# Latent attention: the reciprocals of the softmax sums spread by fp32r products of ones with diagonal blocks

## The chip, the cores and the metric

The kernel is one launch on one core of a Trainium2 chip. What counts is the device time of that launch in microseconds (us). The engines are TensorE (PE in the profile, its weight loads PEld), VectorE (DVE), ScalarE (ACT), GpSimd (POOL) and SyncE (SP, which only starts transfers). Each runs its own list of instructions in order and waits for the others on semaphores.

## The reference

A two-layer backbone over 1024 latent and 256 context tokens of width 1024. Each layer has an input projection, three mixers side by side (a long convolution, a retention, latent attention), an output projection and an MLP. The change is in the attention. Per head (8 heads, keys of 96, values of 64) it computes

```python
s = jnp.einsum('bqhd,bkhd->bhqk', qi, k, preferred_element_type=jnp.float32)
p = jax.nn.softmax(s, axis=-1).astype(v.dtype)
return jnp.einsum('bhqk,bkhd->bqhd', p, v)
```

The latent queries see all 1280 keys. In the first layer alone the context queries are computed too, and they see the 256 context keys. Queries, keys and values of a head come from low-rank inputs by one more matrix product each (`w_uq`, `w_ukv`).

## The kernel before, in words

Every product in full precision is made of fp32r halves: a tensor is split into a high and a low part, and `three_pass` multiplies hi by hi, hi by lo and lo by hi (lines 152 to 154).

`phase_latent` does the attention of a layer. A **unit** is one tile of 128 queries of one head. The units run pair of heads by pair (p = 0 to 3), in it head by head (s = 0, 1), in it tile by tile: 10 tiles in the first layer (t = 8 and 9 are the context tiles, with two key tiles only), 8 in the second, so 80 and 64 units. Two neighbouring units are a **couple** (40 and 32 of them): they share one accumulation with the values. All engines walk over the same step number j, each a fixed distance behind:

- PE, step j: scores of unit j (`score`, lines 152 to 154 with kT and qT), transposes of the exponentials of units j-2 and j-1 (line 2031), and one half of `weigh` of the couple m: half 0 at j = 2m+4, half 1 at the odd step j = 2m+5 (line 2051, 10 products of 128x256 for latent tiles). At the end of half 1 it **spreads the reciprocals**: line 2059 multiplies the broadcast column of 1/sum with the identity, an fp32 product of 64x128 for each of the two units, so that every row of the output block has the reciprocals of its queries. Last it **makes** the next query, key or value chunk, if one stands in the table `made_in` (a deck of 12 makes for the pair to come in the first layer, `k k k q q q v v v q q q`, of 10 in the second). A make fills one of the four PSUM banks in a ring, and `bank_free` waits until what lay there has been read: for a make it is ACT's copy of the make before.
- DVE, step j: row maxima of unit j (line 1923, 1927), the low parts of the transposed probabilities (line 1943), and at odd j = 2m+3 `invert(m)`: the sums of couple m added and inverted (lines 1936 and 1937, names att_sums and att_rinv).
- ACT, step j: high parts of the transposed probabilities (line 1767), then `copy` of the make of step j-1 out of PSUM (line 1748, name make_raw, two buffers, so it waits until GpSimd is through with the make before the last), then at even j = 2m+6 `out(m)`: reciprocals and both value sums out of PSUM (lines 1775 to 1777), and `exp` of unit j (line 1757).
- POOL, step j: at even j = 2m+6 `norm(m)` (lines 1856, 1859), then `split` of the make of step j-1 into its high and low parts (lines 1823 to 1847), and at the third step of a pair `weights(p)`: the split of the raw weights of the next pair (lines 1806 to 1809).
- SP loads the raw weights of the pairs to come into one buffer, and stores the finished pair.

`out(m)` waits for `norm(m-1)`, `weigh` of the next couple waits for `out(m)`, and `score` of the next unit waits for `exp`.

Of the kernel before, what the change touches and what calls it, by code (L numbers as in the profile page):

```python
# [19 lines left out]
F32 = mybir.dt.float32  # L20
# [5 lines left out]
P = 128  # L26
# [1511 lines left out]
def latent_weights(kit, l, q, p):  # L1538
# [3 lines left out]
    uq_raw, ukv_raw = kit.at("uq_raw", [P, 2, LAT_QW], 187 if first else 130), kit.at("ukv_raw", [P, LAT_KVW], 191 if first else 132)  # L1542
# [14 lines left out]
def phase_latent(kit, l):  # L1557
# [15 lines left out]
    uq_raw = [kit.at("uq_raw", [P, 2, LAT_QW], kb) for kb in (187, 130)]  # L1573
    ukv_raw = [kit.at("ukv_raw", [P, LAT_KVW], kb) for kb in (191, 132)]
# [20 lines left out]
    mx = kit.at("att_max", [P, 2, 8], 202.5)  # L1595
    sums, rinv = kit.at("att_sums", [P, 2, SUM_RING], 202.75), kit.at("att_rinv", [P, SUM_RING], 203)
# [30 lines left out]
    for p in range(1, PAIRS):  # L1627
        deck = [("k", p, 0, c) for c in range(3)] + queries(p, 0) + [("v", p, 0, c) for c in range(3)] + queries(p, 1)
        made_in.update({(p - 1) * per_pair + 5 + i: m for i, m in enumerate(deck)})
# [46 lines left out]
    for s in (scored, exped):  # L1676
        s.plan(parts)
    p_turned, p_hi, p_lo = kit.sig("att_p_turned"), kit.sig("att_p_hi"), kit.sig("att_p_lo")
# [20 lines left out]
    with nc.Block() as block:  # L1699
        @block.sync  # L1700
        def _(sp):
            sp.dma_start(rot[MLA_NOPE:P, :], io["rope_rows"]).then_inc(rot_in.sem, 16)
            sp.wait_ge(kr_ready.sem, kr_ready["kr"])
            latent_weights(kit, l, sp, 1)
            n_tok = len(q_tiles) * P
            for p in range(PAIRS):
                if p + 2 < PAIRS:
                    sp.wait_ge(w_lo.sem, w_lo[p + 1])
# [83 lines left out]
        def _(pool):  # L1792
# [56 lines left out]

            def norm(m):  # L1850
# [11 lines left out]
            for j in range(n_units + 5):  # L1862
                if 0 <= j - 6 and j % 2 == 0:
                    norm((j - 6) // 2)
                    own(normed, normed[(j - 6) // 2])
                if j - 1 in made_in:
# [9 lines left out]
        def _(dve):  # L1876
            link = kit.dve_chain.link
            dve.wait_ge(w_hi.sem, w_hi["first"])
# [90 lines left out]
        def _(pe):  # L1969
# [65 lines left out]
            def weigh(m, half):  # L2035
# [17 lines left out]
                if half == 1:  # L2053

                    pe.wait_ge(inverted.sem, inverted[m])
                    r = s * MLA_V
                    for i in range(2):
                        at = (2 * m + i) % SUM_RING
                        last = pe.matmul(psf[r:r + MLA_V, O0 + (2 + i) * P:O0 + (3 + i) * P],
                                         rinv[:, at:at + 1].broadcast_to([P, MLA_V]), kit.ident[:], start=True, stop=True)  # L2060
# [1012 lines left out]
def build(nc, io, phases=None):  # L3073
    with ExitStack() as ctx:
# [6 lines left out]
        kit.ones = kit.small("ones", [P, P])  # L3081
# [6 lines left out]
        kit.ret_pos, kit.ret_lg = kit.small("ret_pos", [P, 4]), kit.small("ret_lg", [P, 8, DEPTH * 2 * RET_H])  # L3088
        kit.ret_dm_dram = nc.dram_tensor("ret_dm_scratch", (DEPTH, P, RET_H, P), F32).ap()
# [131 lines left out]
```

## Time and profile before

| | us |
|---|---|
| median of 3 runs | 3949.2 (3948.46 to 3953.78) |
| the profiled execution, own time | 3948.27 |
| its span in the profile | 3946.4 |
| PE busy (share of the span) | 3643.4 (92%) |
| DVE busy | 2129.9 (54%) |
| ACT busy | 1417.4 (36%) |
| POOL busy | 1366.5 (35%) |

PE is the busiest engine by far: read first where it waits and for whom. The profile is of one execution. Its own time is 1.9 us over its span and 0.9 us under the median. Attention takes about 655 to 1053 us in the first layer and 2626 to 2976 us in the second. A row of the trace gives a start, a duration, an engine, a line, and what is written and read; in square brackets stands how long the engine was idle before it and what ended that. PE's matmuls overlap: what one costs is the distance between two starts, not its duration.

### The profile page before, as it was taken

The page shows a single profiled execution, that of the slowest core. Times are in us where ns is not written, and L with a number is a line of the kernel's source. Part 1 is how long each engine was busy: PE and PEld are TensorE (multiplying, and loading weights), DVE is VectorE, ACT ScalarE, POOL GpSimd, SP SyncE. Part 2 cuts the span into 40 slices and gives each one's busy share as a digit, 9 for nine tenths or more (in the row PEclk, how much of TensorE's full clock was granted, in tenths as well). Part 3 has the DMA queues.
Part 4 walks back from the last instruction along what each step waited for, and adds up shares of the span by engine and source line. Part 5 has one row for each costly group of instructions (what it writes and reads, how often), then busy time and mean ns, then how long its engine had stood idle before and what let it go on. Part 6 is the DMA issues. An engine that isn't in the chain of part 4 may idle for free. (4 is left out here: it accounts for less than half of the span.)

```text
span 3946.4 us, 53247 instructions
## 1 busy us (share of the span) xinstructions
PE 3643.4 (92%) x19584; PEld 3058.6 (78%) x19584; DVE 2129.9 (54%) x3793; ACT 1417.4 (36%) x2845; POOL 1366.5 (35%) x1239
## 2 busy tenths in 40 slices
PE   7989997999779899999999899969996989999997
PEld 3668996777667688888888679958886768888886
DVE  5468435666676444444444583356676555544544
ACT  3341125666513522222222412246672252222222
POOL 1121122555100055454554421126630005544554
PEclk8989977999889999999999899879998999999999
DMA  5245201001324111111111162010014311111111
GB/s 206 104 168 186 82 4 41 12 8 40 122 78 163 43 43 32 32 43 43 43 32 32 69 202 79 4 39 10 6 39 165 150 43 50 52 48 43 53 52 49
DMA packets 153895, 266.96 MB, mean 68 GB/s; under 512 B 8968, under 2 KB 122777, under 8 KB 151290
## 3 DMA queue, kind: packets, MB, share of 16 engines
q1 hardware_dynamic: 143452, 212.38, 16.2%
q0 software_dynamic: 6352, 46.01, 3.0%
q10 hardware_dynamic: 3920, 6.29, 0.5%
q8 instruction: 107, 1.75, 0.2%
q14 instruction: 64, 0.52, 0.0%
HBM read 229.10 MB, written 33.59 MB: 67 GB/s over the span
## 5 line engine op out<-in xcount | busy, mean ns | idle before, releaser
L2990 POOL TENSOR_TENSOR x<-x,mlp_tmp 128x512 f32<-128x512 f32 x576 | 785.3, 1394 | 1323.7 <-DVE mlp_tmp L2971 1318.5
L2971 DVE TENSOR_TENSOR mlp_tmp<-psum,gate 128x512 f32<-128x512 f32 x576 | 391.7, 689 | 273.1 <-POOL x L2990 194.5
L152 PE MATMUL psum<-act_hi,w_hi 128*128 128x512 f32 (+1 forms) x1280 | 472.6, 369 | 14.4 <-DVE w_lo L2949 14.4
L153 PE MATMUL psum<-act_lo,w_hi 128*128 128x512 f32 (+1 forms) x1280 | 472.3, 369 | 0.0
L154 PE MATMUL psum<-act_hi,w_lo 128*128 128x512 f32 (+1 forms) x1280 | 472.1, 369 | 0.0
L152 PE MATMUL psum<-w_hi,hidden_hi 128*128 128x512 f32 x1152 | 449.9, 391 | 0.0
L153 PE MATMUL psum<-w_lo,hidden_hi 128*128 128x512 f32 x1152 | 448.5, 389 | 0.0
L154 PE MATMUL psum<-w_hi,hidden_lo 128*128 128x512 f32 x1152 | 448.3, 389 | 0.0
L2963 DVE TENSOR_TENSOR hidden_lo<-square,hidden_hi 128x512 fp32r<-128x512 f32 x160 | 102.3, 639 | 591.9 <-ACT hidden_hi L2935 591.9
L1923 DVE TENSOR_REDUCE att_max<-psum 128x1 f32<-128x512 f32 (+2 forms) x272 | 217.4, 799 | 259.7 <-PE psum L154 259.5
L2927 ACT ACTIVATE relu<-psum 128x512 f32<-128x512 f32 x160 | 88.8, 555 | 666.0 <-PE psum L154 666.0
L152 PEld LDWEIGHTS psum<-act_hi,w_hi 128*128 128x128 f32 x1280 | 242.2, 189 | 56.0 <-DVE w_lo L2949 15.2
L1757 ACT ACTIVATE probs<-psum,att_max 128x512 f32<-128x512 f32 (+2 forms) x272 | 208.5, 771 | 190.5 <-DVE att_max L1927 189.8
L153 PEld LDWEIGHTS psum<-act_lo,w_hi 128*128 128x128 f32 x1280 | 242.2, 189 | 40.6
L154 PEld LDWEIGHTS psum<-act_hi,w_lo 128*128 128x128 f32 x1280 | 242.2, 189 | 40.3
L152 PE MATMUL psum<-w_in_hi,act_hi 128*128 128x256 f32 (+1 forms) x912 | 259.2, 284 | 0.0
L154 PE MATMUL psum<-w_in_hi,act_lo 128*128 128x256 f32 (+1 forms) x912 | 256.8, 282 | 0.0
L153 PE MATMUL psum<-w_in_lo,act_hi 128*128 128x256 f32 (+1 forms) x912 | 256.8, 282 | 0.0
L152 PEld LDWEIGHTS psum<-w_hi,hidden_hi 128*128 128x128 f32 x1152 | 216.3, 188 | 47.6 <-DVE mlp_tmp L2971 3.6
L154 PEld LDWEIGHTS psum<-w_hi,hidden_lo 128*128 128x128 f32 x1152 | 216.3, 188 | 45.2
L153 PEld LDWEIGHTS psum<-w_lo,hidden_hi 128*128 128x128 f32 x1152 | 216.4, 188 | 43.7
L2923 ACT ACTIVATE w_hi<-w_raw 128x1024 fp32r<-128x1024 f32 x64 | 64.2, 1051 | 467.5 <-PE psum L154 467.5
(386 smaller groups left out, 8238.6 us busy)
## 6 DMA issues: line engine op xcount, KB each, us to landing
w_raw<-in_mlp_w SPq DMA_DIRECT2D x128, 512.0 KB, 3.8
side_w<-in_w_ada SPq DMA_DIRECT2D x40, 1024.0 KB, 6.5
w_raw<-in_w_in SPq DMA_DIRECT2D x32, 512.0 KB, 4.8
hy_ahead<-in_hy_ahead POOLq DMA_DIRECT2D x8, 2048.0 KB, 12.6
open_tab<-in_hy_ahead POOLq DMA_DIRECT2D x8, 1024.0 KB, 13.0
spec_scratch<-open_staged SPq DMA_DIRECT2D x16, 512.0 KB, 2.7
hy_spec<-spec_scratch SPq DMA_DIRECT2D x16, 512.0 KB, 3.5
hy_back<-in_hy_back POOLq DMA_DIRECT2D x2, 4096.0 KB, 29.9
```

Of the source, the lines that this page charges most:

```text
L152: pe.matmul(out, lhs[0], rhs[0], start=start, stop=False)
L153: pe.matmul(out, lhs[0], rhs[1], start=False, stop=False)
L154: return pe.matmul(out, lhs[1], rhs[0], start=False, stop=stop)
L1757: act.activation(pe_[:, n % 2, at:end], psf[:, at:end], ACT.Exp, scale=SCALE, bias=mx[:, n % 2, 1:2], accum_out=sums[:, k, n % SUM_RING:n ...
L1923: dve_last = dve.tensor_reduce(mx[:, n % 2, 6 + k:7 + k], psf[:, at:at + len(part) * P], AX.X, ALU.max)
L2923: act.activation(w2h[:, f], raw2[:, f], ACT.Copy).then_inc(w2_hi.sem, 1)
L2927: act.activation(relu[:, i % 2, 0:n], ps[:, i % 4, 0:n], ACT.Relu).then_inc(relued.sem, 1)
L2963: dve.tensor_tensor(hlo[:, g % 2, f, 0:n], square[:, i % 2, 0:n], hh[:, g % 2, f, 0:n].bitcast(F32), ALU.subtract).then_inc(h_lo.sem, 1)
L2971: dve.tensor_tensor(tmp[:, j % 2, :], ps[:, 4 + j % 4, :], gate[:, int(t >= LAT_TILES), 512 * h:512 * h + 512], ALU.mult).then_inc(gated.s ...
L2990: pool.tensor_tensor(a, a, tmp[:, j % 2, :], ALU.add).then_inc(added.sem, 1)
```

## The change

The two fp32 products of the reciprocals become two fp32r products over both units at once. GpSimd prepares them: `spread(m)` multiplies the identity with each of the two columns of reciprocals (two blocks of 128x128 in one new buffer, `att_diag_full`), copies the 128x256 result into an fp32r high part and subtracts for the low part. PE multiplies a constant matrix of ones with the high and then with the low part. It now waits for `spread(m)` rather than for `invert(m)`. `spread(m)` stands at POOL's odd step j = 2m+3, ahead of the split of that step, and waits for `invert(m)` and for the end of `weigh(m-1)`, since there is one pair of diagonal buffers.

The decks of makes start one step later (6 + i rather than 5 + i). Buffers are moved: the raw weights lie on the bytes that `split` uses for its temporaries, so SP now loads a pair's raw weights only when the last query of the pair before it is split. Maxima, sums, reciprocals and the ones move to the small area, and DVE writes the ones at the start of the phase.

```diff
-    uq_raw = [kit.at("uq_raw", [P, 2, LAT_QW], kb) for kb in (187, 130)]
-    ukv_raw = [kit.at("ukv_raw", [P, LAT_KVW], kb) for kb in (191, 132)]
+    uq_raw = [kit.at("uq_raw", [P, 2, LAT_QW], kb) for kb in (187, 133)]
+    ukv_raw = [kit.at("ukv_raw", [P, LAT_KVW], kb) for kb in (191, 130)]
...
-    mx = kit.at("att_max", [P, 2, 8], 202.5)
-    sums, rinv = kit.at("att_sums", [P, 2, SUM_RING], 202.75), kit.at("att_rinv", [P, SUM_RING], 203)
+    mx, sums, rinv = kit.att_max, kit.att_sums, kit.att_rinv
+    diag = [kit.at(f"att_diag{a}", [P, 2, P], 202 + a, F32R) for a in range(2)]
+    diag_full = kit.at("att_diag_full", [P, 2, P], 131)
...
-        made_in.update({(p - 1) * per_pair + 5 + i: m for i, m in enumerate(deck)})
+        made_in.update({(p - 1) * per_pair + 6 + i: m for i, m in enumerate(deck)})
...
-            sp.wait_ge(kr_ready.sem, kr_ready["kr"])
+            sp.wait_ge(lo_p.sem, lo_p[weights_free(1)])
             latent_weights(kit, l, sp, 1)
...
                 if p + 2 < PAIRS:
-                    sp.wait_ge(w_lo.sem, w_lo[p + 1])
+                    sp.wait_ge(lo_p.sem, lo_p[weights_free(p + 2)])
                     latent_weights(kit, l, sp, p + 2)
...
+            def spread(m):
+                hi, lo = diag
+                at = 2 * m % SUM_RING
+                pool.wait_ge(inverted.sem, inverted[m])
+                if m:
+                    pool.wait_ge(weighed.sem, weighed[m - 1])
+                for i in range(2):
+                    link(pool, pool.tensor_scalar(diag_full[:, i, :], kit.ident[:], rinv[:, at + i:at + i + 1], None, ALU.mult))
+                link(pool, pool.tensor_copy(hi[:], diag_full[:]))
+                pool.tensor_tensor(lo[:], diag_full[:], hi[:].bitcast(F32), ALU.subtract).then_inc(spread_out.sem, 1)
...
+                if 0 <= j - 3 and j % 2 == 1 and j - 2 < n_units:
+                    spread((j - 3) // 2)
+                    own(spread_out, spread_out[(j - 3) // 2])
...
+            link(dve, dve.memset(kit.ones_r[:].bitcast(F32), 1.0))
...
-                    pe.wait_ge(inverted.sem, inverted[m])
-                    r = s * MLA_V
-                    for i in range(2):
-                        at = (2 * m + i) % SUM_RING
-                        last = pe.matmul(psf[r:r + MLA_V, O0 + (2 + i) * P:O0 + (3 + i) * P],
-                                         rinv[:, at:at + 1].broadcast_to([P, MLA_V]), kit.ident[:], start=True, stop=True)
+                    pe.wait_ge(spread_out.sem, spread_out[m])
+                    for a in range(2):
+                        last = pe.matmul(psf[:, O0 + 2 * P:O0 + 4 * P], kit.ones_r[:],
+                                         diag[a][:].rearrange("p i n -> p (i n)"), start=a == 0, stop=a == 1)
                     last.then_inc(weighed.sem, 1)
```

What this moves on PE is seen at the end of step j = 7 of the first layer, where the second half of `weigh(1)` ends. The kernel before:

```order
L2051 MATMUL psum<-probsT_hi_6435,v_parts_6427 128x256
L2051 MATMUL psum<-probsT_lo_6437,v_parts_6427 128x256
L2059 MATMUL psum<-ident,att_rinv_6445 64x128 x2
L152 MATMUL psum<-lat_hi_6143,w_ukv_hi_6420 128x256
L153 MATMUL psum<-lat_lo_6144,w_ukv_hi_6420 128x256
L154 MATMUL psum<-lat_hi_6143,w_ukv_lo_6421 128x256
```

The same place in the changed kernel:

```order
L2070 MATMUL psum<-probsT_hi_6439,v_parts_6431 128x256
L2070 MATMUL psum<-probsT_lo_6441,v_parts_6431 128x256
L2076 MATMUL psum<-att_diag_95_6447,ones_r 128x256
L2076 MATMUL psum<-att_diag_96_6448,ones_r 128x256
L152 MATMUL psum<-lat_hi_6147,w_ukv_hi_6424 128x512
L153 MATMUL psum<-lat_lo_6148,w_ukv_hi_6424 128x512
L154 MATMUL psum<-lat_hi_6147,w_ukv_lo_6425 128x512
```

The two products per couple stay two, of another kind. The make behind them is the second key chunk (512 wide) where it was the third (256 wide): the deck stands one step later.

On POOL the first deck of the first layer begins after `norm(0)` (L1856, L1859). The kernel before, from there to the second norm:

```order
L1856 TENSOR_TENSOR att_o_hi_6440<-att_o_hi_6440,att_o_lo_6441 64x256
L1859 TENSOR_TENSOR att_6426<-att_o_hi_6440,att_rec_6442 64x256
L1830 CAST kT_hi_6424<-make_raw_6431 64x512
L1831 TENSOR_TENSOR kT_lo_6425<-make_raw_6431,kT_hi_6424 64x512
L1832 CAST make_hi_6433<-make_raw_6431 64x512
L1833 CAST kT_hi_6424<-make_hi_6433 64x512
L1834 TENSOR_TENSOR kT_lo_6425<-make_raw_6431,make_hi_6433 64x512
L1830 CAST kT_hi_6424<-make_raw_6430 64x512
```

The same place in the changed kernel:

```order
L1871 TENSOR_TENSOR att_o_hi_6444<-att_o_hi_6444,att_o_lo_6445 64x256
L1874 TENSOR_TENSOR att_6430<-att_o_hi_6444,att_rec_6446 64x256
L1861 TENSOR_SCALAR att_diag_full_6449<-ident,att_rinv 128x128 x2
L1862 CAST att_diag_95_6447<-att_diag_full_6449 128x256
L1863 TENSOR_TENSOR att_diag_96_6448<-att_diag_full_6449,att_diag_95_6447 128x256
L1833 CAST kT_hi_6428<-make_raw_6435 64x512
L1834 TENSOR_TENSOR kT_lo_6429<-make_raw_6435,kT_hi_6428 64x512
L1835 CAST make_hi_6437<-make_raw_6435 64x512
L1836 CAST kT_hi_6428<-make_hi_6437 64x512
L1837 TENSOR_TENSOR kT_lo_6429<-make_raw_6435,make_hi_6437 64x512
L1871 TENSOR_TENSOR att_o_hi_6444<-att_o_hi_6444,att_o_lo_6445 64x256
```

The first spread of the program has one more row ahead of it. Two steps before the place above, in the split of the first pair's queries, the changed kernel's POOL has:

```order
L1850 TENSOR_TENSOR qT_lo_6427<-make_raw_6435,qT_hi_6426 96x512
L1861 ISA
L1861 TENSOR_SCALAR att_diag_full_6449<-ident,att_rinv 128x128 x2
L1862 CAST att_diag_95_6447<-att_diag_full_6449 128x256
L1863 TENSOR_TENSOR att_diag_96_6448<-att_diag_full_6449,att_diag_95_6447 128x256
L1849 CAST qT_hi_6426<-make_raw_6434 96x256
```

The spread stands ahead of the first key split, and one stands ahead of every second split of a deck. The row `ISA` occurs once at line 1861; the kernel before has one of the same kind at line 564, and the profile calls it MODIFY_POOL_CONFIG.

## Rows read from the trace of the kernel before

**Rows 1.** Windows view, 100 us of attention: span, PE, PEld, DVE, ACT, POOL.

```profile
700.00:800.00 100.00, 92.69 (x607) 78.30 (x607) 61.02 (x126) 65.96 (x166) 58.83 (x70) 1.00 0.04 12
```

**Rows 2.** PE's timeline, second layer: end of an odd unit without a make.

```profile
2906.39 0.28 PE L2051 MATMUL psum<-probsT_lo,v_parts 128*128 128x256 f32 x1
2906.60 0.65 PE L2059 MATMUL psum<-ident,att_rinv 128*64 128x128 f32 x4
2907.18 0.50 PE L152 MATMUL psum<-kT_hi,qT_hi 96*128 96x512 f32 x1
```

**Rows 3.** PE's timeline, second layer: starts of the two units before.

```profile
2898.01 0.50 PE L152 MATMUL psum<-kT_hi,qT_hi 96*128 96x512 f32 x1
...
2902.36 0.50 PE L152 MATMUL psum<-kT_hi,qT_hi 96*128 96x512 f32 x1
```

**Rows 4.** ACT's timeline, second layer: start of an `out`, head s = 1.

```profile
2908.82 0.38 ACT L1775 ACTIVATE att_rec<-psum 64x256 f32<-64x256 f32 x1
```

**Rows 5.** POOL by form: one-input and two-input operations; the last column is idle before.

```profile
L1806 POOL CAST w_ukv_hi<-ukv_raw 128x256 fp32r<-128x256 f32 x6 | 2.4, 396 | 0.4
L1807 POOL CAST w_uq_hi<-uq_raw 128x512 fp32r<-128x512 f32 x6 | 3.7, 614 | 0.4
L1808 POOL TENSOR_TENSOR w_ukv_lo<-ukv_raw,w_ukv_hi 128x256 fp32r<-128x256 f32 x6 | 4.4, 736 | 0.5
L1042 POOL CAST lat_hi<-lat_tmp 128x256 fp32r<-128x256 f32 x2 | 1.6, 805 | 2.2 <-ACT lat_tmp L976 2.1
```

**Rows 6.** POOL's timeline, first layer: starts of splits and norms, steps 6 to 16.

```profile
689.01 0.60 POOL L1830 CAST kT_hi<-make_raw 64x512 fp32r<-64x512 f32 x1
...
693.75 0.65 POOL L1830 CAST kT_hi<-make_raw 64x512 fp32r<-64x512 f32 x1
...
700.12 0.39 POOL L1830 CAST kT_hi<-make_raw 64x256 fp32r<-64x256 f32 x1
...
703.12 1.28 POOL L1841 TENSOR_TENSOR make_turned<-make_raw,rope_rows 32x512 f32<-32x512 f32 x1
...
709.23 0.73 POOL L1856 TENSOR_TENSOR att_o_hi<-att_o_hi,att_o_lo 64x256 f32<-64x256 f32 x1
...
710.85 1.26 POOL L1841 TENSOR_TENSOR make_turned<-make_raw,rope_rows 32x512 f32<-32x512 f32 x1
...
742.86 0.73 POOL L1856 TENSOR_TENSOR att_o_hi<-att_o_hi,att_o_lo 64x256 f32<-64x256 f32 x1 [1.91 <-ACT att_o_lo L1777]
```

**Rows 7.** PE's timeline: make of j=6, make of j=7, score(14).

```profile
688.94 0.40 PE L152 MATMUL psum<-lat_hi,w_ukv_hi 128*128 128x512 f32 x1
...
694.88 0.39 PE L152 MATMUL psum<-lat_hi,w_ukv_hi 128*128 128x256 f32 x1
...
726.77 0.44 PE L152 MATMUL psum<-kT_hi,qT_hi 96*128 96x512 f32 x1
```

**Rows 8.** ACT's timeline: copy, exp (j=13), out, exp (j=20).

```profile
723.47 0.62 ACT L1748 ACTIVATE make_raw<-psum 128x512 f32<-128x512 f32 x1
...
725.67 0.69 ACT L1757 ACTIVATE probs<-psum,att_max 128x512 f32<-128x512 f32 x1 [1.57 <-DVE att_max L1927]
...
757.40 0.38 ACT L1775 ACTIVATE att_rec<-psum 64x256 f32<-64x256 f32 x1
...
760.17 0.69 ACT L1757 ACTIVATE probs<-psum,att_max 128x512 f32<-128x512 f32 x1 [1.62 <-DVE att_max L1927]
```

**Rows 9.** ACT's timeline, second layer: exp (j=13), idle time before.

```profile
2698.88 0.69 ACT L1757 ACTIVATE probs<-psum,att_max 128x512 f32<-128x512 f32 x1 [2.08 <-DVE att_max L1927]
```

**Rows 10.** Line 564's pool configuration, and POOL's timeline around its first.

```profile
L564 POOLq MODIFY_POOL_CONFIG  x2: 7/7/7, 59.6 to 59.6; - x2
...
64.43 1.26 POOL L564 TENSOR_TENSOR open_ksum<-open_ksum,open_size 128x512 f32<-128x512 f32 x1 [4.79 <-DVE open_size L658]
```

**Rows 11.** Raw weights' DMA (last number: us to landing); POOL's last query split.

```profile
ukv_raw<-in_mla_w_ukv SPq DMA_DIRECT2D x3, 128.0 KB, 3.6
...
672.23 0.39 POOL L1846 CAST qT_hi<-make_raw 96x256 fp32r<-96x256 f32 x1
```

More of the change, by code:

```diff
@@ L1541, in latent_weights @@
     first = p == 0
-    uq_raw, ukv_raw = kit.at("uq_raw", [P, 2, LAT_QW], 187 if first else 130), kit.at("ukv_raw", [P, LAT_KVW], 191 if first else 132)
+    uq_raw, ukv_raw = kit.at("uq_raw", [P, 2, LAT_QW], 187 if first else 133), kit.at("ukv_raw", [P, LAT_KVW], 191 if first else 130)
     w_raw = kit.sig("lat_w_raw", 16)
@@ L1677, in phase_latent @@
         s.plan(parts)
+    spread_out = kit.sig("att_spread")
+    spread_out.plan(range(n_couples))
     p_turned, p_hi, p_lo = kit.sig("att_p_turned"), kit.sig("att_p_hi"), kit.sig("att_p_lo")
@@ L3080, in build @@
         kit.stat = kit.small("stat", [P, 4, 20])
-        kit.ones = kit.small("ones", [P, P])
+        kit.ones = kit.small("ones", [P, 8])
         kit.mla_gain = kit.small("mla_gain", [P, 3])
@@ L3088, in build @@
         kit.ret_pos, kit.ret_lg = kit.small("ret_pos", [P, 4]), kit.small("ret_lg", [P, 8, DEPTH * 2 * RET_H])
+        kit.att_max, kit.att_sums, kit.att_rinv = (kit.small(n, s) for n, s in (
+            ("att_max", [P, 2, 8]), ("att_sums", [P, 2, 8]), ("att_rinv", [P, 8])))
+        kit.ones_r = kit.small("ones_r", [P, P], F32R)
         kit.ret_dm_dram = nc.dram_tensor("ret_dm_scratch", (DEPTH, P, RET_H, P), F32).ap()
```

## The prediction

> **What bounds the kernel now.** I read the windows of the attention first: in 100 us of the first layer PE is busy 92.7 us, ACT 66, DVE 61, POOL 59 [rows 1]. PE bounds, but with gaps, so I read its timeline unit by unit, and then the engines that end its gaps. Two sorts of units without a make show. The odd unit from 2902.36 to 2907.18 takes 4.82 us, the even one before it 4.35 [rows 2, 3]. In the odd one PE works through and ends with line 2059. In the even one it waits near the end for ACT's exponentials: its length is the loop of score, maximum, exp and the next score, and PE's work is not its limit. So work taken off PE counts only in odd units. In units with a make (a deck is 12 of 20 units in the first layer, 10 of 16 in the second) PE takes up the slack, and ACT still idles 1.6 to 2.1 us ahead of its exp, waiting for the maximum [rows 8, 9]. Between those moments stands POOL: in the first deck it goes from split to split without a gap (689.01, 693.75, 700.12 after a norm, 703.12 [rows 6]), and a split begun late would hold ACT's copies. That is where the change has to be weighed.
>
> **PE, the products.** From the last product of line 2051 to the next score are 0.79 us [rows 2]. Neighbouring 128x256 products in that accumulation start 0.12 apart, so line 2059 costs 0.67 per couple. The new pair is two fp32r products with 256 columns, of the form of its neighbours: 0.24. That is 0.43 less per couple, 72 couples, at most 31.0 us. Three couples of the first layer and one more at its end stand behind context units, where the odd unit is already down to 4.34: nothing to win (-1.7). In the heads with s = 1, ACT's move of the output stands just before the exp of the even unit (2908.82 [rows 4]); with an odd unit that is shorter, ACT comes to that exp later in the unit, and part is given back. I estimate 0.12 per couple of s = 1, which makes 4.2 over 35 of them. Left are **-25.1 us**: 14.1 in the first layer, 11.0 in the second. That is the price if nothing else is late.
>
> **POOL, the spread.** No spread is in the trace. One-input operations took 0.396 us for 128x256 and 0.614 for 128x512, so 0.85 ns per element of a row; 128x128 would be 0.29 [rows 5]. Two of them 0.58, the copy 0.40, the subtraction 0.74, four gaps of 0.08: **2.1 us per couple**. From below: at half the 128x256 row each, 1.9. From above: tensor_scalar reads a scalar per partition, which no row shows; at half the two-input row it is 0.37 each, which gives 2.2. The dearest row of a 128x256 copy is 0.805 [rows 5]; with the first three operations at that height (two at 0.4 and one at 0.8, the blocks scaled) and the subtraction at 1.2 it comes to 3.1. I take 2.1, since most rows of POOL in this phase stand at the low price. POOL has 41 us free in 100 and gets about 20 us more work. The mean is not the question; the decks are.
>
> **The first layer's decks.** Anchor: the end of `weigh(1)` at j = 7, the make behind it starts at 694.88 [rows 7]. `spread(2)` of j = 7 must wait for just this (one pair of diagonal buffers), and behind it in POOL's order stands the split of K chunk 0, now made at j = 6. From the rows 6: K 512 wide 4.74, K 256 wide 3.0, a query split 6.1, a norm 1.6. POOL from the anchor: 0.3 until it starts, spread 2.1, K0 4.74, norm 1.6, K1 4.74, spread 2.1, K2 3.0, norm 1.6, Q0 6.1, spread 2.1, Q1 6.1: 34.5 us, with no gap to catch up in. ACT's copy of V0, at j = 13, has two raw buffers and must wait for the split of Q1. It takes 0.6, and exp(13) stands behind it. score(14) follows exp(13) by 1.1 (725.67 to 726.77 [rows 7, 8]). So score(14) stands at anchor + 36.3. Before it was 726.77 - 694.88 = 31.9, and PE alone would make it 30.4 (three couples less 0.43, and 0.2 from the key chunks' other places). The loss against PE alone is **5.9 us a deck**. In the kernel before, that copy began at 723.47, ahead of exp by 2.2, and waited for nobody.
>
> A second place is j = 20. `out(7)` waits for `norm(6)`, which stands in POOL's order at j = 18, behind Q0 and Q1 of the other head with a spread between them. From the norm at 742.86 [rows 6]: 1.6, 6.1, 2.1, 6.1, 1.6 = 17.5, so 760.4 where `out` began at 757.40 [rows 8]: 3.0 late. From its end to exp(20) were 1.6 free (758.6 to 760.17), so 1.4 reach score(21), and the two gains of the couples in between, 0.8, are lost too: 2.2. Together 8.1 per deck, 24.3 in three decks. First layer: 24.3 - 14.1 = **+10.2**.
>
> **The second layer's decks.** The same chain of 34.5 applies, but there are no short context units at j = 8 and 9, so ACT's slots lie later, and 2.1 us of slack stood ahead of the exp at j = 13 [rows 9]. I find the copies at most 2.3 late, of which about 0.75 passes through: 2.3 in three decks. Second layer: 2.3 - 11.0 = **-8.7**.
>
> **The rest.** A norm or a spread that comes later is not waited for elsewhere: `weigh` needs its spread two units after the maximum, 3 us of slack or more in the first layer, 0.8 in the second. In the first steps the spread of j = 3 goes ahead of the last query split (672.23 [rows 11]), and SP loads the next raw weights only after this split: 672.2 + 2.1 + 1.2 = 675.5, landing 3.6 [rows 11] and issue 0.9, 3.2 for POOL's weight splits: 683.2, while PE's K0 make is due at about 688.5 [rows 7]. The pool configuration at line 1861 is new. Line 564 has one: set at 59.6, and POOL's next operation at 64.43, just after DVE's [rows 10]. So it costs between 0 and 4.8; with 4.8 the weights are ready at 688.0, still in time. I put 0.5 for this and for DVE's write of the ones, between 0 and 3. In the later pairs the raw weights come 10 steps ahead of their use.
>
> The Trainium skill, "GPSIMD Engine Reference", § 2.1 Instruction dispatch, says that the first call into a freshly loaded library pays some 6 us for its code. The trace bounds it to 4.8 here. By the page the weights would be 1.2 later than by my upper bound, about 0.7 us of stall once; nothing of the sum changes its sign by it.
>
> **Sum.** +10.2 - 8.7 + 0.5 = +2.0 against the profiled execution's 3948.3: 3950.3. The median of the runs stands 0.9 above that execution: **3951.2 us**. It is a small difference of two large terms. The chain on POOL may be off by 1 us per deck, the gain on PE by 0.08 per couple, 6 us each: own range 3942 to 3961.
>
> **Rivals.**
> (1) POOL hides the spread. The decks' delays are taken up by ACT's and DVE's idle time, because copies and `out` can slip inside a unit. For it: POOL is free 41% of the time, and ACT idles 1.6 ahead of exp(13). Against it: that idle time is a third of the delay, and POOL has no gap in the deck. Time: 3948.3 - 25.1 + 0.5 + 0.9 = 3924.6; halfway, 3938.
> (2) The spread is dearer, and this ends slower. POOL's chain carries three spreads in a deck of the first layer and about 2.5 in one of the second, where the slack is then used up: 16.5 us of time for each us of price. From 2.5 us per spread the kernel is slower by more than the bound. At the upper end of 3.1 the time is 3951.2 + 16.5 = 3968. For it: the copy of 0.805 [rows 5], and POOL's operations would be beside more DVE work. Against it: the splits' copies in attention stand at 0.60 for 512 columns [rows 6].
> (3) The fp32r pair costs what line 2059 costs, as it waits for its weights or for the spread. Then the gain goes and the decks stay: about 3975. The neighbours of the same form at 0.12 speak against it.
>
> **How the numbers follow.** No change is within 0.2%, 7.9 us: 3941.3 to 3957.1. The forecast has 0.56 (0.02 of it faster, 0.42 the same, 0.12 slower). Rival 1 has 0.22, 0.20 of it faster and 0.02 the same. Rival 2 has 0.18: 0.16 slower, 0.02 the same. Rival 3 has 0.04, slower. Sum: faster 0.22, same 0.46, slower 0.32. The range takes in the halfway case of rival 1 and rival 2 up to 3.0: 3936 to 3967.
>
> **What the profile will show.** The new products start 0.12 apart, 144 of them, and the odd unit without a make falls from 4.82 to 4.39. The spread's four operations take 2.1 us from start to end. POOL's busy time in 100 us of the first layer goes from 59 to about 80. ACT's copies (none waited for POOL before) wait for it at j = 10, 12 and 13 of the first layer's decks, and `out` at j = 20. A period of the first layer (20 units) becomes longer by about 3.4 us where it has a deck, one of the second (16 units) shorter by about 2. I am wrong if copies at j = 13 do not wait, if the spread takes over 2.5 us, or if the odd unit does not fall.

## The result, and the profile after

| | before | changed |
|---|---|---|
| median of 6 runs, us | 3950.6 (3948.5 to 3953.8) | 3973.8 (3965.5 to 3980.5) |
| ratio, 95% interval | | 1.0057 (1.0041 to 1.0073) |
| span of the profiled execution | 3946.4 | 3976.1 |
| first layer, score(0) to score(79) | 387.0 | 414.5 |
| second layer, score(0) to score(63) | 333.2 | 334.2 |

The kernel became slower by 23 us, 0.6%. The profiled execution shows 29.7 us more, and all but 1.1 of it lies in the two attention stretches: 27.6 in the first layer, 1.0 in the second. They are measured on PE's timeline, from the start of the first score of the first unit to that of the last. The six times of the changed kernel lie in two groups, 3965.5 to 3969.7 us and 3977.9 to 3980.5 us, the first at a slightly higher mean clock (0.942 to 0.945 against 0.939), and the profiled execution is of the second, 4 us above the median.

The windows of 100 us, in the columns of [rows 1] (the number behind POOL's is the granted clock, 1.00 for 2.4 GHz), for the changed kernel; the last is a stretch of 6 us behind a stall:

```profile
700.00:800.00 100.00, 86.64 (x529) 75.80 (x530) 54.28 (x112) 59.73 (x149) 76.32 (x101) 0.91 0.03 11
819.00:825.00 6.00, 5.82 (x19) 5.05 (x20) 0.00 (x0) 2.66 (x7) 5.33 (x10) 0.50 0.00 0
```

POOL went from 59 to 76 of 100 us and PE from 93 to 87. The granted clock, 1.00 before, is 0.91 in the mean, and in the six microseconds behind a wait it is 0.50, which is 1.2 GHz. Over the whole first stretch TensorE ran at 1.2 GHz for 64 us in this execution (mean granted clock 0.92), against 10 us in the kernel before (0.99).

POOL's instructions by form, the spread's three lines:

```profile
L1861 POOL TENSOR_SCALAR att_diag_full<-ident,att_rinv 128x128 f32<-128x128 f32 x144 | 87.1, 605 | 153.2 <-DVE att_rinv L1956 80.5 <-PE psum L2076 63.4
L1863 POOL TENSOR_TENSOR att_diag<-att_diag_full,att_diag 128x256 fp32r<-128x256 f32 x72 | 52.7, 733 | 6.2
L1862 POOL CAST att_diag<-att_diag_full 128x256 fp32r<-128x256 f32 x72 | 28.6, 397 | 4.9
```

A tensor_scalar of 128x128 took 0.605 us. I had 0.29 from the copies [rows 5] and 0.37 as the upper estimate from two-input rows. The other two are as forecast. A spread is 2.6 us, not 2.1.

The second deck of the first layer on POOL's timeline. Only the row that begins each piece stands here (spread, key split, norm, key split, spread, short key split, norm, query split, spread, query split, norm):

```profile
803.88 1.30 POOL L1861 TENSOR_SCALAR att_diag_full<-ident,att_rinv 128x128 f32<-128x128 f32 x2 [5.49 <-PE psum L2076]
...
806.52 0.61 POOL L1833 CAST kT_hi<-make_raw 64x512 fp32r<-64x512 f32 x1
...
811.26 0.73 POOL L1871 TENSOR_TENSOR att_o_hi<-att_o_hi,att_o_lo 64x256 f32<-64x256 f32 x1
...
812.87 0.60 POOL L1833 CAST kT_hi<-make_raw 64x512 fp32r<-64x512 f32 x1
...
817.61 1.30 POOL L1861 TENSOR_SCALAR att_diag_full<-ident,att_rinv 128x128 f32<-128x128 f32 x2
...
820.25 0.39 POOL L1833 CAST kT_hi<-make_raw 64x256 fp32r<-64x256 f32 x1
...
823.25 0.72 POOL L1871 TENSOR_TENSOR att_o_hi<-att_o_hi,att_o_lo 64x256 f32<-64x256 f32 x1
...
824.86 1.26 POOL L1844 TENSOR_TENSOR make_turned<-make_raw,rope_rows 32x512 f32<-32x512 f32 x1
...
830.97 1.30 POOL L1861 TENSOR_SCALAR att_diag_full<-ident,att_rinv 128x128 f32<-128x128 f32 x2
...
833.63 1.27 POOL L1844 TENSOR_TENSOR make_turned<-make_raw,rope_rows 32x512 f32<-32x512 f32 x1
...
839.70 0.71 POOL L1871 TENSOR_TENSOR att_o_hi<-att_o_hi,att_o_lo 64x256 f32<-64x256 f32 x1
```

The first spread waits 5.49 us for the products of `weigh` before it, and behind it POOL goes for 36 us without a gap: the chain of the prediction, piece by piece. ACT's timeline where it waits for this chain (the copies of Q0 at j = 10 and V0 at j = 13, `out` at j = 20, in the second period):

```profile
817.60 0.60 ACT L1751 ACTIVATE make_raw<-psum 128x512 f32<-128x512 f32 x1 [4.56 <-POOL kT_lo L1837]
...
839.71 0.60 ACT L1751 ACTIVATE make_raw<-psum 128x512 f32<-128x512 f32 x1 [3.49 <-POOL qT_lo L1850]
...
876.04 0.38 ACT L1778 ACTIVATE att_rec<-psum 64x256 f32<-64x256 f32 x1 [3.19 <-POOL att L1874]
```

They answer to [rows 8], where none waits for POOL. And PE's timeline behind the first of them, from the stall to where the clock is back:

```profile
819.18 0.58 PE L2070 MATMUL psum<-probsT_hi,v_parts 128*128 128x256 f32 x1 [3.21 <-ACT att_o_lo L1780]
...
823.61 0.63 PE L154 MATMUL psum<-lat_hi,w_uq_lo 128*128 128x512 f32 x1
824.04 0.63 PE L152 MATMUL psum<-kT_hi,qT_hi 96*128 96x512 f32 x1
...
825.53 0.40 PE L153 MATMUL psum<-kT_lo,qT_hi 96*128 96x512 f32 x1
825.76 0.39 PE L154 MATMUL psum<-kT_hi,qT_lo 96*128 96x512 f32 x1
```

PE waits 3.21 us, and its products of 512 columns then follow each other at 0.43 us (823.61 to 824.04), against 0.23 once the clock is back (825.53 to 825.76). That costs time which the wait itself does not show.

What the change was to bring is there as well. PE's timeline at the end of an odd unit of the second layer, the place of [rows 2]:

```profile
2982.79 0.28 PE L2070 MATMUL psum<-probsT_lo,v_parts 128*128 128x256 f32 x1
2982.91 0.40 PE L2076 MATMUL psum<-att_diag,ones_r 128*128 128x256 f32 x2
2983.14 0.48 PE L152 MATMUL psum<-kT_hi,qT_hi 96*128 96x512 f32 x1
```

From the last product of `weigh` to the next score are 0.35 us where there were 0.79.

### The profile page after: what moved, and what is told of

Its sections match the earlier page's. It is cut to its first block and busy times, and to the rows that moved or that the text cites. A ratio compares the mean times of both kernels' runs of the same rounds, so it can differ in the third digit from the quotient of the medians.

```text
span 3976.1 us, 53327 instructions
## 1 busy us (share of the span) xinstructions
PE 3633.5 (91%) x19440; PEld 3063.9 (77%) x19440; DVE 2124.9 (53%) x3795; ACT 1422.2 (36%) x2845; POOL 1540.3 (39%) x1527
## 5 line engine op out<-in xcount | busy, mean ns | idle before, releaser
L154 PEld LDWEIGHTS psum<-w_hi,hidden_lo 128*128 128x128 f32 x1152 | 216.3, 188 | 45.1
```

The lines of the kernel that those rows point to most:

```text
L154: return pe.matmul(out, lhs[1], rhs[0], start=False, stop=stop)
```

## The experiments

Theory A was that POOL's spread makes the splits of the decks late, and that the clock adds to each stall. The rivals: B, the later decks and the moved loads are what costs; C, the new products save nothing; E, it is the amount of POOL's work and not its place; D, DVE's work lengthens the loop of score, maximum and exp. All intervals below are of the ratio to the kernel before, from runs on the same chip; the rows come from several chips, on which the kernel before had 3949.5 to 3951.3 us. The two stretches are of one profiled execution each. "First" and "second" are the two attention stretches, as in the table above.

| kernel | median us | ratio, 95% interval | first | second |
|---|---|---|---|---|
| changed | 3973.8 | 1.0041 to 1.0073 | 414.5 | 334.2 |
| decks later only | 3951.0 | 0.9993 to 1.0012 | 385.3 | 333.3 |
| no spread | 3919.4 | 0.9900 to 0.9933 | 369.4 | 321.6 |
| one product on POOL | 3947.0 | 0.9986 to 1.0005 | 394.6 | 324.0 |
| spread behind the split | 3949.5 | 0.9988 to 1.0007 | 397.6 | 320.3 |
| both of these | 3932.4 | 0.9935 to 0.9964 | 382.3 | 320.0 |
| PE's waits filled | 3965.3 | 1.0029 to 1.0063 | 401.4 | 332.7 |
| POOL's spread, old products | 3981.4 | 1.0062 to 1.0091 | 410.7 | 337.3 |
| spread on DVE | 3992.0 | 1.0096 to 1.0139 | 414.8 | 346.6 |
| two wide fp32r products | 3964.6 | 1.0019 to 1.0047 | 398.3 | 335.6 |
| one wide fp32 product | 3921.1 | 0.9917 to 0.9950 | 373.9 | 322.8 |
| the same, with a copy | 3919.8 | 0.9912 to 0.9939 | 372.7 | 322.8 |

**Decks later only.** In the kernel before:

```diff
-        made_in.update({(p - 1) * per_pair + 5 + i: m for i, m in enumerate(deck)})
+        made_in.update({(p - 1) * per_pair + 6 + i: m for i, m in enumerate(deck)})
```

> The kernel before with its decks one step later (6 + i for 5 + i) and nothing else. Theory A (the spread on POOL makes the splits late, and TensorE runs at half clock behind the stalls): no difference, 3946 to 3955 us. Theory B (the later deck is what costs, the spread only comes with it): 3960 to 3975 us, with ACT's copies at j = 13 waiting for POOL here too.

3951.0 us, no difference. B has lost its first half: the step by which the decks are later costs nothing by itself.

**No spread.** The changed kernel, with POOL's call of `spread` gone and

```diff
+            for a in range(2):
+                link(dve, dve.memset(diag[a][:].bitcast(F32), 1.0))
...
-                    pe.wait_ge(spread_out.sem, spread_out[m])
+                    pe.wait_ge(inverted.sem, inverted[m])
```

> The changed kernel with its later decks, moved buffers and fp32r products, but POOL writes no diagonal: DVE sets both buffers to 1.0 once, so the reciprocals are left out of the output, and the products wait for invert. Theory A: the gain on PE alone; couples without a make 8.6 us for 9.15 before, no copy waits for POOL, granted clock 1.00 in the decks, 3915 to 3928 us. Theory B (later decks, later weight loads): the stalls stay, 3955 to 3975 us. Theory C (the new products themselves cost as much as the old): 3945 to 3955 us.

3919.4 us, with the reciprocals left out of the output. B and C are both out: with later decks, later weight loads and the new products, the kernel is 30 us faster than before. The two stretches are 29.2 us shorter (17.6 and 11.6). So what the products give is 29 us, and what the spread on POOL takes is 45.1 + 12.6 = 58 us.

**One product on POOL.**

```diff
-                for i in range(2):
-                    link(pool, pool.tensor_scalar(diag_full[:, i, :], kit.ident[:], rinv[:, at + i:at + i + 1], None, ALU.mult))
+                link(pool, pool.tensor_tensor(diag_full[:], bcast(kit.ident[:], 1, 2), bcast(rinv[:, at:at + 2], 2, P), ALU.mult))
```

> The changed kernel with one POOL tensor_tensor of 128x256 (identity and reciprocals both repeated by stride 0) where two tensor_scalar of 128x128 stood: two operations of 0.605 and a gap become one of about 0.73, so a spread takes 2.1 us for 2.65. Theory A: 0.55 us less per spread in POOL's chain is 1.6 per deck of the first layer and its stalls (3.2, 2.0, 2.9 us) each get shorter by about as much: 3953 to 3966 us. Theory B: no change against the changed kernel, 3968 to 3980 us.

3947.0 us: better than expected by 6 us or more, and level with the kernel before. The product is cheaper than I expected. POOL's timeline of this kernel, one spread and what follows:

```profile
704.09 0.61 POOL L1860 TENSOR_TENSOR att_diag_full<-ident,att_rinv 128x256 f32<-128x256 f32 x1
704.77 0.40 POOL L1861 CAST att_diag<-att_diag_full 128x256 fp32r<-128x256 f32 x1
705.24 0.72 POOL L1862 TENSOR_TENSOR att_diag<-att_diag_full,att_diag 128x256 fp32r<-128x256 f32 x1
706.03 0.40 POOL L1833 CAST kT_hi<-make_raw 64x256 fp32r<-64x256 f32 x1
```

The one product of 128x256 took 0.61 us, as long as each tensor_scalar of half its size, so this spread is 1.94 us (704.09 to 706.03), 0.70 under the changed kernel's 2.64 and 0.16 under what I had predicted for the change. The loss against no spread falls from 45.1 to 25.2 in the first layer and from 12.6 to 2.4 in the second, 30 us in the two profiled executions and 24 us by the ratios of all runs, for 0.70 us of a spread. Theory A holds, but I had the slope too small.

**Spread behind the split.** The two calls in POOL's step change places:

```diff
-                if 0 <= j - 3 and j % 2 == 1 and j - 2 < n_units:
-                    spread((j - 3) // 2)
-                    own(spread_out, spread_out[(j - 3) // 2])
                 if j - 1 in made_in:
                     split(made_in[j - 1])
                     own(lo_p, lo_p[made_in[j - 1]])
+                if 0 <= j - 3 and j % 2 == 1 and j - 2 < n_units:
+                    spread((j - 3) // 2)
+                    own(spread_out, spread_out[(j - 3) // 2])
```

> The changed kernel with POOL's spread behind the split of its odd step, not ahead of it. POOL's chain loses one of three spreads ahead of V0's copy and starts 3 us earlier, since the split of K0 no longer waits for the end of weigh(1). Theory A: the waits of the first layer's decks shrink by 3 to 5 us each, 3940 to 3962 us. Rival E (what hurts is the amount of POOL work, not where it stands): 3968 to 3980 us. A third outcome: TensorE's products wait for the diagonals in the decks, since a split of 6 us now stands ahead of them.

3949.5 us, inside what theory A gave, and against E: the same instructions in another order take 24 us less. The second layer's loss is gone (320.3 against 321.6 without a spread). In the first layer units 12 and 13 still take 8.8 and 7.6 us.

**Both together.** The one product and the changed places, 3932.4 us:

> Both repairs of POOL's part together: the spread of three operations (one product of 128x256, 2.1 us) and behind the split of its step. Each alone took 24 to 27 us off the changed kernel and left waits in the first layer alone (394.6 and 397.6 us there against 369.4 without a spread). Theory A: POOL's chain in a deck is 0.56 shorter three times and starts earlier, most waits are gone: 3922 to 3940 us. If the wait of units 12 and 13 (8.8 and 7.6 us with the spread behind the split) is for the diagonals behind Q's split, it stays: 3942 us or more.

It is faster than the kernel before by 0.5%. PE's timeline in the second deck shows what is left: `out` is late at 815.62, and at 822.26 the products wait for the diagonals themselves.

```profile
815.62 0.39 PE L2069 MATMUL psum<-probsT_hi,v_parts 128*128 128x256 f32 x1 [1.28 <-ACT att_o_lo L1780]
...
822.26 0.51 PE L2075 MATMUL psum<-att_diag,ones_r 128*128 128x256 f32 x2 [1.16 <-POOL att_diag L1862]
```

**PE's waits filled.** In the first layer, ahead of the wait for `out` at j = 10 of each deck (24 products) and at j = 20 and 40 (22):

```diff
+            def fill(j, count):
+                item = ring[ring_at[(j - 1, min(1, len(turned_parts(j - 1)) - 1))] + 1]
+                bank_free(item)
+                for _ in range(count):
+                    pe.matmul(bank_of(item)[:, 0:256], kit.ones_r[:], ch[:, 2, 0:256], start=True, stop=True)
```

> The changed kernel, and TensorE has 24 (steps 10 of each deck) or 22 (steps 20 and 40) products of 128x256 into the next free bank of the ring to do where it stood idle for 3 us waiting for ACT's out, in the first layer only; nothing reads them. They are work of 2.9 and 2.6 us that only replaces idle time. Theory A with the clock (the stalls cost more than their length, since the granted clock is 1.2 GHz for 5 to 6 us behind each): the clock stays at 2.4 GHz behind them, units 20 and 21 get 2 to 3 us shorter per place, of the deck's part some is hidden by POOL: 3956 to 3968 us. Without it (the low clock costs nothing, all is POOL's chain): 3973 us or more.

3965.3 us, inside what the theory with the clock gave. That number alone shows no gain: the interval of its ratio, 1.0029 to 1.0063, overlaps the changed kernel's, 1.0041 to 1.0073. What the filling does is read from the places themselves. PE does 116 more products there. Windows of this kernel and then of the changed one, the 10 us that hold the wait at j = 20:

```profile
760.00:770.00 10.00, 9.66 (x72) 9.03 (x71) 4.85 (x12) 4.15 (x12) 7.93 (x12) 1.00 0.13 39
```

```profile
760.00:770.00 10.00, 7.09 (x49) 6.60 (x48) 4.68 (x11) 5.35 (x16) 9.14 (x12) 0.86 0.06 11
```

The clock stays at 1.00 where it fell to 0.86. Units 20 and 21 take 10.4 us for 13.0, and so do units 40 and 41, the same place one pair later; without a spread they take 8.3. So of 4.7 us lost at each such place 2.6 are the clock's, and 2.1 are POOL's chain. At j = 10 the filling only moves the wait to unit 12 (8.4 to 8.8 us for 4.9 to 5.9): from the make of j = 7 to score(14) the later decks take 38.4 us with it and 38.2 without. What is gained there is 0.9 us a deck, unit 14 back at full clock (5.3 us for 6.3), and 2.4 us in the first deck, where the clock had also been low in unit 13.

The first stretch is 13 us shorter in all, but the five filled places account for only 9 of it. Another 3.0 us is unit 4, ahead of all of them (4.35 us for 7.30). Both kernels do the same there, and PE waits 1.2 us for the exponentials in both, but the clock fell in one execution only:

```profile
671.60 0.77 PE L152 MATMUL psum<-kT_hi,qT_hi 96*128 96x512 f32 x1 [1.20 <-ACT probs L1760]
```

```profile
673.01 0.50 PE L152 MATMUL psum<-kT_hi,qT_hi 96*128 96x512 f32 x1 [1.21 <-ACT probs L1760]
```

The first row is of the changed kernel, the second of the one with filled waits. The waits at j = 13 and at j = 60 were not filled.

**POOL's spread, old products.**

```diff
-                    pe.wait_ge(spread_out.sem, spread_out[m])
+                    pe.wait_ge(inverted.sem, inverted[m])
```

and the two fp32 products of line 2059 below it.

> The changed kernel's POOL spread, decks and buffers, with TensorE's two fp32 products of before, which wait only for invert: nobody reads the diagonals. Loss without gain. Theory A: the couples outside the decks go back to 9.15 us for 8.62, and in the decks POOL is the bound and PE's work counts little: 3980 to 4000 us. If gain and loss only add: 3974 + 29 = 4003 us.

3981.4 us, only 7.6 over the changed kernel, with intervals that overlap (1.0062 to 1.0091 against 1.0041 to 1.0073): the difference may be anything from nothing to 16 us. It is not the 29 us of the sum, so gain and loss do not add. The products give 29 us without the spread, and at most about half of that beside it. The stretches are of no help here: the profiled execution of this kernel was its shortest (span 3970.9), that of the changed kernel one of its longer ones.

**The price of tensor_scalar.** One run, which leaves the reciprocals of the even units out of the output:

```diff
-                for i in range(2):
-                    link(pool, pool.tensor_scalar(diag_full[:, i, :], kit.ident[:], rinv[:, at + i:at + i + 1], None, ALU.mult))
+                link(pool, pool.tensor_scalar(diag_full[:, 0, :], kit.ident[:], 0.001, None, ALU.mult))
+                link(pool, pool.tensor_scalar(diag_full[:, 1, :], kit.ident[:], rinv[:, at + 1:at + 2], None, ALU.mult))
```

> Of the changed kernel's two POOL tensor_scalar of 128x128 the first takes a constant as its scalar (so the reciprocals of even units are left out of the output), the second a column, as before. If the column costs, the first takes 0.3 us, as copies of POOL do per element, and the second 0.605; if the operation itself is dearer than a copy, both take 0.6. The time is of no matter: near the changed kernel's, or 10 to 20 us less if the first is cheap.

It took 3969.2 us, inside the range of the changed kernel's times. Its POOL instructions by form:

```profile
L1861 POOL TENSOR_SCALAR att_diag_full<-ident,att_rinv 128x128 f32<-128x128 f32 x72 | 43.3, 602 | 6.8
L1860 POOL TENSOR_SCALAR att_diag_full<-ident 128x128 f32<-128x128 f32 x72 | 38.1, 530 | 139.4 <-DVE att_rinv L1957 78.8 <-PE psum L2077 58.1
```

The larger part of the price is the operation's and not the column's: 0.530 with a constant, 0.602 with a column of SBUF. Per element of a row this is 4.7 ns, against 2.9 for a product of two tiles (0.733 for 256) and 1.5 for a copy (0.397 for 256).

This kernel is the changed one but for 0.08 us per spread, and its profiled execution had 37 us at 1.2 GHz in the first stretch where the changed kernel's had 64. That stretch took 405.1 us against 414.5. At 34 us per us of spread, the slope found below, 0.08 makes about 3 us (an estimate), so some of the 414.5 belongs to that one execution and not to the kernel.

**Spread on DVE.** POOL's spread goes, DVE does after its reciprocal:

```diff
+                for i in range(2):
+                    link(dve, dve.tensor_scalar(hi[:, i, :], kit.ident[:], rinv[:, at + i:at + i + 1], None, ALU.mult))
+                for i in range(2):
+                    last = dve.scalar_tensor_tensor(out=lo[:, i, :], in0=kit.ident[:], scalar=rinv[:, at + i:at + i + 1],
+                                                    in1=hi[:, i, :].bitcast(F32), op0=ALU.mult, op1=ALU.subtract)
```

> The changed kernel with the spread on DVE behind its reciprocal: two tensor_scalar of 128x128 write the high parts, two scalar_tensor_tensor of 128x128 write the low parts (identity times reciprocal less the high part), about 1 us on an engine that is busy 61 of 100 us. POOL gets back its order of before. Theory A: near the kernel without a spread, 3918 to 3935 us. Rival D (DVE's maxima sit in the loop of score, maximum, exp, so anything on DVE lengthens each couple): 0.5 to 1 us for each of 72 couples above that, 3955 us or more.

3992.0 us, the slowest of all: theory A's figure was wrong by 57 us. The timelines of DVE and POOL of this kernel, in one deck:

```profile
713.26 2.07 DVE L1941 TENSOR_SCALAR att_diag<-ident,att_rinv 128x128 fp32r<-128x128 f32 x2 [1.09 <-PE psum L2075]
713.98 1.26 POOL L1844 TENSOR_TENSOR make_turned<-make_raw,rope_rows 32x512 f32<-32x512 f32 x1
715.32 1.26 POOL L1845 TENSOR_TENSOR make_raw<-make_raw,rope_rows 32x512 f32<-32x512 f32 x1
715.37 2.70 DVE L1943 SCALAR_TENSOR_TENSOR att_diag<-ident,att_rinv,att_diag 128x128 fp32r<-128x128 f32 x2
716.66 1.25 POOL L1846 TENSOR_TENSOR make_raw<-make_raw,make_turned 32x512 f32<-32x512 f32 x1
```

and where POOL is idle:

```profile
728.04 0.61 DVE L1941 TENSOR_SCALAR att_diag<-ident,att_rinv 128x128 fp32r<-128x128 f32 x2
728.69 0.61 DVE L1943 SCALAR_TENSOR_TENSOR att_diag<-ident,att_rinv,att_diag 128x128 fp32r<-128x128 f32 x2
```

The same four instructions take 1.22 us alone and 4.8 us beside POOL's splits; the second pair ends when the row of POOL at 716.66 ends. Each of the four ends 0.08 to 0.15 us behind the POOL instruction that ran beside it. Behind them stands the maximum that the next exp needs, and unit 12 of a deck is 9.7 us long (4.9 without a spread). So D's price is right and its mechanism is for the most part another: not DVE's work, but its waits for POOL. The edit also makes DVE wait, in its own order, for the end of `weigh` (1.09 in the first row, 20.3 us in the whole kernel); no run parts the two.

The Trainium skill, "SBUF — State Buffer", § SBUF: two separate sides, says that DVE and GpSimd share one pair of ports as a lock held for a whole instruction, and that an operation of DVE in a 2-port mode, or one with two SBUF inputs, contends for it with a GpSimd operation that reads SBUF; these rows agree, 4.8 us for 1.2. The tensor_scalar here has one tile and one column as inputs and waits too (2.07 for 0.61); no run shows in which mode it ran.

**Without diagonals.** One fp32 product can give both units' reciprocals, if DVE writes each column 64 times:

```diff
-                dve.reciprocal(rinv[:, at:at + 2], total).then_inc(inverted.sem, 1)
+                dve.reciprocal(wide[m % 2][:], bcast(total, 2, MLA_V)).then_inc(inverted.sem, 1)
...
+                    last = pe.matmul(psf[:, O0 + 2 * P:O0 + 3 * P], wide[m % 2][:].rearrange("p i n -> p (i n)"), kit.ident[:],
+                                     start=True, stop=True)
```

> No diagonals at all. DVE's reciprocal writes each of the couple's two columns 64 times (128 numbers a row instead of 2), and one fp32 product of 128x128 (these 128 columns as weights, the identity streamed) gives both units' reciprocals, those of the second in rows 64 to 127; ACT moves them out in two pieces of 64x128. Full precision, no spread on POOL; decks and buffers as in the changed kernel. One fp32 product instead of two: 0.33 us less per couple on PE; nothing late on POOL. Theory A: 3925 to 3935 us. If ACT's extra instruction or DVE's wider reciprocal sits in the loop of score, maximum and exp, 0.2 to 0.4 a couple are given back: 3940 to 3950 us.

3921.1 us, 0.7% under the kernel before and 53 us under the changed one; it is 4 us better than expected. PE's timeline at the end of a `weigh` of the second layer, from a variant with the same product (next paragraph):

```profile
2704.42 0.28 PE L2056 MATMUL psum<-probsT_lo,v_parts 128*128 128x256 f32 x1
2704.54 0.39 PE L2061 MATMUL psum<-ident,att_wide 128*128 128x128 f32 x2
2704.75 0.49 PE L152 MATMUL psum<-kT_hi,qT_hi 96*128 96x512 f32 x1
```

A product of fp32 with all 128 columns of weights is recorded as two (x2). From the last product of `weigh` to the next score are 0.33 us, so it costs 0.21 here (0.14 ahead of a make), no more than the fp32r pair's 0.23. The two of the kernel before, each with 64 columns of weights, are four records and 0.67 us [rows 2]. The whole saving was to be had in full precision.

```diff
-                dve.reciprocal(wide[m % 2][:], bcast(total, 2, MLA_V)).then_inc(inverted.sem, 1)
+                link(dve, dve.reciprocal(rinv[:, at:at + 2], total))
+                dve.tensor_copy(wide[m % 2][:], bcast(rinv[:, at:at + 2], 2, MLA_V)).then_inc(inverted.sem, 1)
```

> The kernel with one wide fp32 product, but DVE inverts two columns (0.165 us) and a copy repeats them 64 times, where the reciprocal of 128 numbers a row took 0.952 us. If DVE's time there sits in the loop of score, maximum and exp (units 4.78 and 5.33 against 4.58 and 5.00 without a spread), about 0.3 us per couple come back, 20 us at most less what the copy takes: 3905 to 3920 us. If that copy waits for POOL's instructions, as DVE's products of two tiles in SBUF did: 3920 to 3945 us.

The reciprocal of 128 numbers a row took 0.953 us; two numbers and a copy take 0.165 + 0.228. That variant comes to 3919.8 us, no difference: this part of DVE is not in the loop. Its copy took 0.228 in the median, 0.398 in the mean and 1.204 at worst:

```profile
L1942 DVE COPY att_wide<-att_rinv x72: 226/228/1204, 672.2 to 2943.4; 128x128 f32<-128x128 f32 x72
```

The stretches stay 4.5 us longer than with no spread. ACT's second instruction may be the cause, which is not tested: the even units whose `out` is of a head s = 1 take 4.78 us for 4.58.

And with the columns split for fp32r, against the kernel with one wide product:

```diff
...
+                link(dve, dve.reciprocal(wide_full[:], bcast(total, 2, MLA_V)))
+                link(dve, dve.tensor_copy(hi[:], wide_full[:]))
+                dve.tensor_tensor(lo[:], wide_full[:], hi[:].bitcast(F32), ALU.subtract).then_inc(inverted.sem, 1)
...
```

> As the kernel with one wide product, but DVE splits the 128 columns into an fp32r high and low part (two more short operations), and TensorE does two fp32r products of 128x128 with an fp32r copy of the identity. At 0.12 each that is 0.43 less per couple than before, 0.1 better than one fp32 product: 3918 to 3928 us by theory A. If DVE's second operation of two SBUF inputs waits for POOL as the diagonals did on DVE, 3930 to 3950 us.

Two fp32r products with the 128 columns split by DVE give 3964.6 us. DVE's subtraction reads two tiles of SBUF and took 0.555 us in the mean, 0.29 in the median and 1.39 at worst, which fits waits for POOL as the spread on DVE had them. The time is above the upper end that I had for it, and no run shows that these waits are all of it. Unit 8 of a deck takes 6.3 to 6.9 us for 4.7 with one wide product.

## Why the prediction was wrong

The mechanism and the places in the decks were right. Two terms of the sum were too small, the spread's price and what a us of it costs, and the time (3951.2) stands 22.6 under the measured one, outside the range.

- **PE's products.** Forecast -25.1 us, measured -29.2 (14.1 and 11.0 against 17.6 and 11.6). The neighbours' spacing of 0.12 was the right price. The odd units without a make fell as forecast (4.82 to 4.37). Inside the decks an odd unit fell by 0.54 and not 0.43 (6.75 to 6.21 at unit 9 of the second layer); why is not shown. Of the 17.6 us, 1.7 are seen with the later decks alone.
- **The spread's price: the first step that failed.** I took 2.1 us, "since most rows of POOL in this phase stand at the low price", and gave 2.2 as what half of a two-input row makes. It was 2.6: two operations of 0.605, dearer per element than any row that I drew on. A bound from another operation's rows was no bound. The price of 3.1, which I kept for the range, covered it; with my slope it gives 3968, and the measured 2.64 gives 3960. So the price accounts for 9 of the 22.6 us. The sign that I had named, a spread of over 2.5 us, is the one that came.
- **The slope: the second step that failed.** I had 16.5 us per us of spread. From 1.94 to 2.64 us the kernel took 24 us more by the ratios of all runs, 34 per us, where my slope has 12. That is most of what the price leaves. In the two profiled executions the stretches grew by 20.0 and 10.1 us, but 3.0 of the 20.0 is the clock at unit 4 (4.34 and 7.30 us), where the spread has no part. What the rest is:
  - In the decks of the first layer, from the make of j = 7 to score(14), 2.2 us more for 0.70: each us passes three times, as forecast.
  - At j = 20, 3.5 us more in the later decks. I had summed the waits at their length and put the clock at nothing. The filled waits show that 2.6 of the 4.7 us lost there are the clock's. Behind the wait at j = 13 unit 14 takes 6.3 us for 5.3 in the same way.
  - In the second layer 2.2 us a deck, in units 10 and 12 to 14, so each us passes 3.1 times where I had 2.5. The other 3.0 us stand at units 51 and 52, a place that I did not have. POOL issues two DMAs between the last split and the spread, PE waits for the diagonals, and there the clock falls once more for 3.4 us (POOL's timeline, then PE's):

```profile
2933.74 0.82 POOL L2128 DMA_DIRECT2D hy_in<-hy_scratch  x1 [0.30 <-POOL qT_lo L1850]
2935.14 1.33 POOL L1861 TENSOR_SCALAR att_diag_full<-ident,att_rinv 128x128 f32<-128x128 f32 x2
...
2937.80 0.57 PE L2076 MATMUL psum<-att_diag,ones_r 128*128 128x256 f32 x2 [1.83 <-POOL att_diag L1863]
```

- **Near the predicted price.** With 1.94 us my sum gives 3948.6, and 3947.0 was measured. That is partly luck: the loss was 27.6 us where the sum has 24.0, and the products gave 29.2 where it has 25.1.
- **Decks, first layer.** score(34) was forecast at anchor + 36.3 and stands at 841.76 - 803.51 = 38.3; three spreads at 0.5 more account for 1.6 of the 2.0. The copies at j = 10 and 13 and `out` at j = 20 wait for POOL as forecast; that at j = 12 waits in the first of these decks only. The periods of 20 units with a deck grew by 7.6 to 8.9 us where I had 3.4, and the later ones of the second layer became 0.6 shorter, not 2.
- **The rest.** The pool configuration cost nothing on the path: it was set at 670.95, and the spread's first operation began at 671.53, after 0.54 us of idle time that ended with DVE's reciprocal. So neither the 4.8 us nor the 6 us that I had weighed was paid. The later decks cost nothing.
- **The rivals.** Rival 2, the dearer spread, is what happened, and I gave it 0.18. "From 2.5 us per spread the kernel is slower by more than the bound" was right at 2.6. Rival 3 (dear products) and rival 1 (hidden by POOL's idle time) are out by the runs without a spread.

## What to carry to other kernels

An engine with 40% of its time free can still be the one without a gap in the stretch that matters, so new work on it is priced there, in its own order, not in its mean. A price taken from another operation of the same engine is a guess; where a sum of two large terms hangs on it, its cheapest form should be tried first (here two halves of one product against one whole). Before a product is moved to another format, look at its shape: the weights' other half was free. And before a difference of two traces is given to an edit, look at a place that the edit does not touch: here 3 us of 13 stood in one.

## What the runs showed of the hardware

- POOL's tensor_scalar of 128x128 takes 0.60 us with a column and 0.53 with a constant, a copy of twice the size 0.40 and a subtraction of two tiles of twice the size 0.73; the product of the identity with a column repeated by stride 0, twice the size, 0.61.
- In the first layer a wait of PE of 2 to 3 us is followed by 3 to 7 us at 1.2 GHz. Products that nobody reads, in place of the wait, kept 2.4 GHz and made two units 2.6 us shorter; that the whole kernel gains is not shown. The same wait of 1.2 us was followed by 1.2 GHz in one execution and not in another.
- DVE's reciprocal takes 0.165 us for two numbers a row and 0.953 for 128, a copy of 128 takes 0.228.
- DVE's operations on two tiles of SBUF, and its tensor_scalar with a column, took up to 1.41 and 1.33 us while POOL computed, and 0.35 and 0.29 alone.
- One fp32 product with 128 columns of weights costs PE 0.14 to 0.21 us, two with 64 each 0.67.
